# Hybrid decoder block on one core: the mean square of x taken from the transposed x

## What is computed

```
def rmsnorm(x, w):
    return x * rsqrt(mean(x * x, axis=-1) + EPS) * w      # x: 256 tokens x 1024

h = rmsnorm(x, norm_mix)
proj = h @ w_in          # split: q, six kv heads, gates, retention q ("qr"), k, v, ...
```

## Time and profile before

| | |
|---|---|
| time, median of 3 (lowest, highest) | 472.08 us (471.12, 472.64) |
| span of the profiled execution | 469.9 us |
| TensorE busy | 438.6 us, 93% |
| VectorE busy | 193.7 us, 41% |
| ScalarE busy | 76.9 us, 16% |
| GpSimd busy | 23.4 us, 5% |
| moved by DMA | 150.79 MB, mean 321 GB/s |

### The profile page before, as it was taken

How to read it: one execution, slowest core, us unless ns; L and a number is a source line. 1 busy time by engine, 2 the same in 40 slices (tenths; PEclk the granted TensorE clock), 3 DMA queues, 4 the chain that set the end, 5 groups by cost and what they waited for, 6 DMA issues and landing times.

```text
span 469.9 us, 5881 instructions
## 1 busy us (share of the span) xinstructions
PE 438.6 (93%) x2326; PEld 241.9 (51%) x2326; DVE 193.7 (41%) x430; ACT 76.9 (16%) x209; POOL 23.4 (5%) x44
## 2 busy tenths in 40 slices
PE   8999999999999999999999998999999767958983
PEld 7799885555455555454444775353543421413331
DVE  1683047836975758778831243110201100200113
ACT  1000131423062111110012341010110100101113
POOL 2020000310000010100002110000000000000000
PEclk9999999999999999999999999999999995996998
DMA  8999557508407107969499899999999999999993
GB/s 286 425 423 366 198 173 310 227 0 339 199 0 280 78 1 280 412 270 424 179 389 423 340 369 375 420 430 434 415 436 427 416 431 421 435 430 425 423 413 117
DMA packets 25388, 150.79 MB, mean 321 GB/s; under 512 B 5484, under 2 KB 7949, under 8 KB 18446
## 3 DMA queue, kind: packets, MB, share of 16 engines
q1 hardware_dynamic: 19152, 145.02, 75.0%
q10 hardware_dynamic: 6206, 5.36, 3.5%
HBM read 147.75 MB, written 2.62 MB: 320 GB/s over the span
## 4 chain that ended last, share of the span: by engine, by line
PE 82%; DMA 14%; DVE 1%; ACT 1%; issue 1%; ACTq 0%; SPq 0%; DVEq 0%; POOL 0%
PE bank L741 34%; PE bank L716 33%; DMA spare<-in_moe_gate_up 7%; DMA ring<-in_moe_gate_up 5%; PE bank L1164 5%; PE bank L1146 4%; PE bank L747 2%; PE bank L796 2%; DMA ring<-in_dense 2%; ACT nsa L1597 1%; PE bank L1303 1%; ACT cst L1597 0%; DVE hT_and_y L2213 0%; DVE nsa L2144 0%; PE bank L1215 0%
## 5 line engine op out<-in xcount | busy, mean ns | idle before, releaser
L741 PE MATMUL bank<-ring,x 128*128 128x512 f32 x128 | 57.4, 594 | 0.0
L2153 DVE SCALAR_TENSOR_TENSOR wr<-cst,bank 128x256 f32<-128x256 f32 x8 | 3.4, 421 | 98.2 <-ACT cst L1604 98.2
L741 PE MATMUL bank<-ring,hT_and_y 128*128 128x512 f32 x96 | 43.5, 597 | 0.0
L716 PE MATMUL bank<-ring,nsa 128*32 128x512 f32 x304 | 38.1, 641 | 4.7 <-DMA ring<-in_moe_gate_up 4.3
L716 PE MATMUL bank<-hT_and_y,ring 128*128 128x256 f32 x192 | 42.3, 380 | 0.0
L1164 PE MATMUL bank<-selection,Tb 128*128 128x128 f32 x256 | 33.7, 284 | 5.9 <-ACT cst L1597 5.8
L716 PEld LDWEIGHTS bank<-hT_and_y,ring 128*128 128x128 f32 x192 | 36.2, 190 | 5.7 <-DVE hT_and_y L1690 0.6
L1164 PEld LDWEIGHTS bank<-selection,Tb 128*128 128x128 f32 x256 | 30.4, 194 | 15.8 <-issue 15.7
L741 PEld LDWEIGHTS bank<-ring,x 128*128 128x128 f32 x128 | 23.8, 190 | 27.1 <-issue 27.0
L2144 DVE COPY nsa<-bank 128x512 f32<-128x512 f32 (+1 forms) x20 | 12.5, 625 | 56.0 <-PE bank L1164 30.5
L741 PEld LDWEIGHTS bank<-ring,hT_and_y 128*128 128x128 f32 x96 | 17.6, 190 | 20.3 <-issue 20.3
(11 more groups left out here) (258 smaller groups left out, 625.6 us busy)
## 6 DMA issues: line engine op xcount, KB each, us to landing
ring<-in_moe_gate_up SPq DMA_DIRECT2D x18, 2048.0 KB, 18.3
ring<-in_dense SPq DMA_DIRECT2D x17, 2048.0 KB, 9.1
spare<-in_moe_gate_up SPq DMA_DIRECT2D x4, 2048.0 KB, 20.2
hT_and_y<-in_moe_gate_up SPq DMA_DIRECT2D x4, 2048.0 KB, 23.2
vr_and_gr<-in_moe_gate_up SPq DMA_DIRECT2D x3, 2048.0 KB, 24.8
nsa<-in_moe_down SPq DMA_DIRECT2D x11, 512.0 KB, 15.1
windows<-in_moe_down SPq DMA_DIRECT2D x7, 512.0 KB, 14.4
qkT<-in_moe_down SPq DMA_DIRECT2D x7, 512.0 KB, 14.8
```

What stands on the lines that cost most here:

```text
L716: return nc.tensor.matmul(o, l, r, start=s, stop=e)
L741: ins = nc.tensor.matmul(o, l[:, k, :], r[:, k, :], start=first and k == 0, stop=last and k == n - 1, skip_group_check=True)
```

## The change

The load of x at the start is left out; only the later one is left. The mean square comes from xT instead:

- ScalarE squares each part of xT as it lands, with scale 1/32 before squaring (so the 1024 squares add up to a mean), into `xT_squared`, 8 chunks of 256 columns in the region that holds v later. The first three stand before the small loads of ACT's queue, the last two after them.
- VectorE adds the eight chunks to one in four instructions: chunks 2-3 onto 0-1, 6-7 onto 4-5, 4-5 onto 0-1, 1 onto 0. The first stands between its weighting of parts 3 and 4, the other three after that of part 4.
- TensorE sums over the partitions by token: two matmuls with the summed squares as weights and one column of ones (job `ms`, put in bank 0 outside the turn). They stand before k=5. `R` stands before k=7, as before.
- VectorE adds EPS while it takes `ms` from PSUM; GpSimd's `rstd(0)` waits for that and now stands before its copy of the bias table's rows.
- `xw` is written to a region of its own, so xT stays as it is; `diag` moves to the other half of its region.

```diff
@@ -93,7 +93,7 @@
-JOBS = (["qr0", "R", "qr1", "btab"]
+JOBS = (["qr0", ("ms", 0), "R", "qr1", "btab"]
         + ["kvcT", "ksT", "vs", "kwT", "vwg", "qT0", "qT1"]
@@ -133,8 +133,13 @@
 LAST_N = [0] * NBANK
-for _i, _job in enumerate(JOBS):
-    _b = (_i + BANK0) % NBANK
+_i = 0
+for _job in JOBS:
+    if isinstance(_job, tuple):
+        _job, _b = _job
+    else:
+        _b = (_i + BANK0) % NBANK
+        _i += 1
     if _job is None:
@@ -291,9 +296,11 @@
         squared = pair_a[:, 2048:4096].rearrange("p (t d) -> p t d", t=TT)
-        xw = Tb[:, :].rearrange("p (k t) -> p k t", k=KT)
+        xT = Tb[:, :].rearrange("p (k t) -> p k t", k=KT)
+        xw = pair_a[:, 2048:4096].rearrange("p (k t) -> p k t", k=KT)
+        xT_squared = pair_b[:, 0:2048].rearrange("p (k t) -> p k t", k=KT)
         x_squared = cst[:, C_ROT + D:C_ROT + D + 512]
-        diag = vr[:, 0, 0:TT * P]
+        diag = gr[:, 0, 0:TT * P]
         h_sums = x[:, :, :].rearrange("p t (s k n) -> p (t s) k n", s=2, k=4)
@@ -302,6 +309,7 @@
         s_first = [sem(f"first_block_part{i}") for i in range(len(FIRST))]
+        s_xsq, s_xadd = sem("xT_part_squared"), sem("xT_squares_added")
         s_xw, s_diag, s_ones, s_h = sem("x_weighted"), sem("rstd_diagonal"), sem("ones_ready"), sem("h_ready")
@@ -467,9 +475,6 @@
             for i, ks in enumerate(FIRST):
-                if i == len(FIRST) - 1:
-                    for t in range(TT):
-                        sp.dma_start(x[:, t, :], a["x"][0, t * P:(t + 1) * P, :]).then_inc(s_x[t], 16)
                 w = slice(KT + ks[0] * S if i else 0, KT + (ks[-1] + 1) * S)
@@ -627,9 +632,7 @@
-            def rstd(n, col):
-                pool.wait_ge(s_rs, n)
+            def rstd(col):
                 pool.tensor_tensor(st[:, col + 32:col + 34], st[:, col:col + 2],
@@ -638,9 +641,10 @@
             pool.memset(Pc[:, :, :, :], NEG).then_inc(s_ms, 1)
+            pool.wait_ge(*is_emptied("ms"))
+            rstd(0)
             pool.wait_ge(s_tab, 32)
             pool.tensor_copy(relb_rep, relb.unsqueeze(2).broadcast_to((BUCKETS + 1, HEADS, P // HEADS))).then_inc(s_rep, 1)
-            rstd(1, 0)
             pool.wait_ge(*is_emptied("kvcT"))
...
@@ -797,18 +802,27 @@
                         done(f"qr{i}", ins)
+            def token_squares():
+                o = begin("ms")
+                pe.wait_ge(s_xadd, 4)
+                for t in range(TT):
+                    ins = mm(o[:, t:t + 1], xT_squared[:, 0, t * P:(t + 1) * P], ones[:, 0:1], True, True)
+                done("ms", ins)
+            def spread_rstd():
+                o = begin("R")
+                for t in range(TT):
+                    pe.wait_ge(s_diag, t + 1)
+                    ins = mm(o[:, t * P:(t + 1) * P], ones[:, :], diag[:, t * P:(t + 1) * P], True, True)
+                done("R", ins)
             for i, ks in enumerate(FIRST):
...
                 for k in ks:
-                    if k < KT - 1:
-                        raw_queries(k)
-            o = begin("R")
-            pe.wait_ge(s_ones, 1)
-            for t in range(TT):
-                pe.wait_ge(s_diag, t + 1)
-                ins = mm(o[:, t * P:(t + 1) * P], ones[:, :], diag[:, t * P:(t + 1) * P], True, True)
-            done("R", ins)
-            raw_queries(KT - 1)
+                    if k == 5:
+                        token_squares()
+                    if k == KT - 1:
+                        spread_rstd()
+                    raw_queries(k)
@@ -1377,11 +1391,20 @@
+            def xT_squares(i):
+                ks = slice(FIRST[i][0], FIRST[i][-1] + 1)
+                act.wait_ge(s_xT[i], 16)
+                nc.scalar.activation(xT_squared[:, ks, :], xT[:, ks, :], ACT.Square, scale=D ** -0.5).then_inc(s_xsq, 1)
+            for i in range(3):
+                xT_squares(i)
             act.wait_ge(s_first[2], 16)
...
             act.dma_start(relb[0:BUCKETS, :], a["rel_bias"]).then_inc(s_tab, 16)
+            for i in range(3, len(FIRST)):
+                xT_squares(i)
             o = take("btab")
@@ -1670,16 +1693,23 @@
                 for k in FIRST[i]:
-                    tsc(xw[:, k, :], xw[:, k, :], norm_cols[:, k:k + 1], None, ALU.mult, ALU.bypass).then_inc(s_xw, 1)
-            for i in range(len(FIRST) - 1):
+                    tsc(xw[:, k, :], xT[:, k, :], norm_cols[:, k:k + 1], None, ALU.mult, ALU.bypass).then_inc(s_xw, 1)
+            def add_squares(k, n, m):
+                V.tensor_tensor(xT_squared[:, k:k + n, :], xT_squared[:, k:k + n, :], xT_squared[:, m:m + n, :], ALU.add).then_inc(s_xadd, 1)
+            for i in range(4):
                 weighted_x(i)
-            for t in range(TT):
-                dve.wait_ge(s_x[t], 16)
-                ins = V.tensor_tensor_reduce(gr[:, t, :], x[:, t, :], x[:, t, :], 1.0, 0.0, ALU.mult, ALU.add,
-                                             st[:, 200 + t:201 + t])
-            link(ins)
-            tsc(st[:, 0:2], st[:, 200:202], 1.0 / D, EPS, ALU.mult, ALU.add).then_inc(s_rs, 1)
-            weighted_x(len(FIRST) - 1)
+            dve.wait_ge(s_xsq, 3)
+            add_squares(0, 2, 2)
+            weighted_x(4)
+            dve.wait_ge(s_xsq, len(FIRST))
+            add_squares(4, 2, 6)
+            dve.wait_ge(s_xadd, 2)
+            add_squares(0, 2, 4)
+            dve.wait_ge(s_xadd, 3)
+            add_squares(0, 1, 1)
+            o = take("ms")
+            freed("ms", tsc(st[:, 0:2], o[:, 0:2], EPS, None, ALU.add, ALU.bypass))
             dve.wait_ge(s_rstd, 1)
@@ -2043,7 +2073,7 @@
                 take(piece)
-                dve.wait_ge(s_x[t], 32)
+                dve.wait_ge(s_x[t], 16)
                 xx = x[:, t, c0:c1]
```

More of the change, by code:

```diff
@@ L675, in _ @@
             for i in range(4):
-                rstd(2 + i, 8 + 4 * i)
+                pool.wait_ge(s_rs, i + 1)
+                rstd(8 + 4 * i)
             def weighted(piece):
@@ L682, in router_rstd @@
             def router_rstd(t):
-                pool.wait_ge(s_rs, 6 + t)
+                pool.wait_ge(s_rs, 5 + t)
                 pool.tensor_tensor(st[:, 36 + t:37 + t], st[:, 4 + t:5 + t], st[:, 250:251], ALU.pow).then_inc(s_rstd, 1)
@@ L693, in _ @@
             for t in range(TT):
-                pool.wait_ge(s_rs, 8 + t)
+                pool.wait_ge(s_rs, 7 + t)
                 pool.tensor_tensor(st[:, 38 + t:39 + t], st[:, 6 + t:7 + t], st[:, 250:251], ALU.pow).then_inc(s_rstd, 1)
```

## The result

The changed kernel takes 473.00 us at the median (471.97 to 475.27), the kernel before 472.59 in the runs beside it; the ratio is 1.0022, with a 95% interval of 1.0012 to 1.0032. The medians lie 0.4 us apart, the means of the runs (473.3 and 472.4) 0.9. The ratio makes it 1.04 us more (0.6 to 1.5), which lies within the 0.3% that the prediction called no change, and on the side it gave. The execution profiled took 473.11 us, with a span of 471.3; the one of before had a span of 469.9.

The account below looks back on a forecast made before the run. TensorE's chain (82% of the span) was taken as the bound. Standstill, `ms` and the removed gap put k=6 at 17.29 instead of 16.29 us, +1.00; span 469.9 + 1.0 = 470.9, plus 2.2 outside it: 473.1 us, range 471.2 to 474.7.

Parts of the forecast that it names:

- TensorE's chain, read in the first 22 us: All edits lie before 22 us on TensorE's chain; the shift there, +1.00 us, passes whole to the end.
- Where the last xT part lands: Behind part four on SP's queue: lands at 10.30 + 2.11 = 12.41 us, bounds 12.2 and 12.8.
- Square and adds: After the last xT part: ScalarE's square 0.60 us, then VectorE's three adds 0.72 + 0.72 + 0.42, to 14.97 us.
- The standstill: TensorE, before `ms` and k=5, waits 0.82 us for the adds, from 14.20 to 15.02 us.
- The removed half: Early x loads, square sums and scaling go: VectorE's 0.36 us gap before k=6 goes; sooner landings costed at nothing.
- From `ms` to R: Scaling, GpSimd's power and diagonals, 1.87 us before, hide under k=5 and 6: diagonals at 17.4, wanted at 19.0.
- GpSimd's order: Power before the copy of the bias table: 16.4 us without an engine's delay, bias product due at 21.2; covered.
- Rival B: Bias table late: 13 small rows an engine behind 16 KB rows, 20.6 us against 21.2 due; up to 474.5; chance 0.04.
- Rival A: Squares later still, TensorE waits longer before k=5: last xT part after 12.83 us; middle 474.3; chance 0.20.
- Rival C: No standstill before k=5, squares in time (landing by 11.6 us, or shorter adds): +0.18 us, 472.1; chance 0.12.
- Rival E: TensorE's clock falls to 1.2 GHz after the standstill; k=5 and 6 need 3.4 us more: 476.5; chance 0.04.
- Rival D: DMA as a whole sets the end, so 1 MB less saves 2.5 us: 469.6; chance 0.05.

Follow-up runs that it names:

- e3: The kernel before with 23 products of ones (46 records) added before k=5; ratio to the kernel before 1.0102 (1.0079 to 1.0125).
- e5: The kernel before without the early loads of x and the sums of squares, mean squares set to 1; ratio to the kernel before 1.0111 (1.0079 to 1.0144).
- e8: The changed kernel with GpSimd's copy of the bias table put before the power again; ratio to the kernel before 1.0065 (1.0040 to 1.0090).
- e10: As e5, with the three small loads on SP's queue, behind the identity and ahead of kv0; ratio to the kernel before 0.9997 (0.9984 to 1.0010).
- e2: The changed kernel with `ms` before k=4 in place of k=5; ratio to the kernel before 1.0067 (1.0041 to 1.0093).
- e4: The changed kernel with x's two early loads kept, behind the last part of xT on SP's queue; ratio to the kernel before 1.0010 (0.9990 to 1.0031).
- e1: The changed kernel with `ms` before k=6 in place of k=5; ratio to the kernel before 1.0009 (0.9994 to 1.0025).
- e6: The changed kernel with R before k=6 in place of k=7; ratio to the kernel before 1.0014 (0.9993 to 1.0035).
- e7: As e5, with the three small loads issued ahead of the fifth weight part on ACT's queue; ratio to the kernel before 1.0058 (1.0039 to 1.0077).

## Why the prediction was right, point by point

- **The number.** Forecast 473.1, measured 473.0: that close is luck. The kernel before had a median of 472.08 in the three runs that the forecast started from and of 472.59 in the 22 beside the changed kernel; and of the 1.04 us of the ratio (forecast 1.00) the front accounts for 0.54. Right are the side, the place and the size within a factor of two. By its own words the prediction would be wrong if TensorE had no wait before k=5, and two of five profiles have none.
- **TensorE's chain, read in the first 22 us.** Right: all of the change that can be placed lies there, and e3 shows that a shift there reaches the end. The profiles of e5 and e8 don't match their ratios as well (3.2 us at the front against 3.7 to 6.8, and 4.8 against 1.9 to 4.3), as each is one execution of six.
- **Where the last xT part lands.** Forecast 12.41, measured 11.99 (12.07, 12.12 and 12.03 in the three that wait), and this is most of what was off in the end of the adds, 14.97 against 14.54. The parts came 1.92 us apart (10.07 to 11.99), which is the 1.9 us that the shares gave; the text had the right arithmetic and then took 2.11 from the row of another pair. Part four was also 0.23 sooner than before.
- **Square and adds.** Right: 0.63 for 0.60, three adds in 1.88 for 1.86.
- **`ms`.** From its first weight load at 14.59 to k=5 at 15.09 are 0.50 us, forecast 0.54. k=6 came at 15.09 + 1.73 = 16.82, 0.53 after the 16.29 of the earlier trace rows. That is the 0.54 us of the first projection. The forecast 15.56 for k=5 is 0.47 more, of which the landing is 0.42. In this one profile TensorE itself was there no sooner, so an even earlier landing would have won nothing.
- **The standstill.** Forecast 0.82, measured none in two profiles and 0.20 to 0.54 in three, with k=5 at nearly the same place: what counts is when the adds are through or TensorE is there, whichever is later, and not how long TensorE stood. The start's pace, which the earlier trace rows doesn't show, decides how much of it is seen. Adding a measured standstill to the length of TensorE's work would mislead here.
- **The removed half.** VectorE's hold on k=6 is gone (0.36 us in the first profile of the kernel before, 0.24 in the second), as forecast. What that is worth depends on the start: R at 17.36 (e10) or, but for its pause, 18.0 (e5), against 18.09 before. R at 18.63 in the changed kernel then puts the added half at 1.27 us in an execution that starts like e10's and at 0.6 in one like e5's. The hold on k=2 until 9.01, which the prediction kept, isn't part of it: the second profile of the kernel before has none.
- **From `ms` to R.** Right that it hides: 15.5 to 16.7 (forecast 17.4), under k=5 and 6. From R to the first projection are 3.18 us before, after and in e10, so nothing changed there. The prediction's 0.2 us by which hT is late against the bias product is less than 0.1: the earlier trace rows has hT through at 21.22, and TensorE's chain goes on at 21.27.
- **GpSimd's order.** Wrong in its price. It was costed at nothing, and the copy of the table was looked at only for the bias product's sake. In fact the change itself pushes the copy from 15.95 to 19.67, and without the new order the power would be behind it (e8: 3.1 us over the kernel before in place of about 1). The new order isn't free of effect: it saves some 2 us.
- **Rival B** had the mechanism right: 13 small rows beside 16 KB rows, forecast 20.6, measured 19.6. It misses the bias product (20.89) by under a microsecond, as forecast. What it didn't ask is who else stands behind that landing.
- **Rival A** didn't happen (the part would have had to land 0.84 later than it did). **Rival C**, no standstill, did happen in two profiles, but not by its way: the squares weren't sooner than 11.6 us, TensorE was late. **Rival E** is real in the executions profiled with 2.24 and 2.58 us of standstill (e8, e2), absent with 3.03 (e5), and absent at 0.5. **Rival D**: the 2.5 us for the missing 1 MB are not won at the end (e10: at most 0.8).

**What stays open.** The ratio is 1.04 us up (0.6 to 1.5), the front 0.54, so the rest may be as little as 0.1. In the profiles the expert stage, where DMA is busy without a break, lies further back than the front explains. TensorE waits there for `vr_and_gr` (start, us, what, idle before); first the kernel before, its second profile, then the changed kernel:

```profile
...
367.74 1.92 PE L716 MATMUL bank<-vr_and_gr,nsa 128*32 128x512 f32 x16 [2.02 <-DMA vr_and_gr<-in_moe_gate_up]
...
```

```profile
...
368.34 1.92 PE L716 MATMUL bank<-vr_and_gr,nsa 128*32 128x512 f32 x16 [2.71 <-DMA vr_and_gr<-in_moe_gate_up]
...
```

```profile
...
369.06 3.35 PE L721 MATMUL bank<-vr_and_gr,nsa 128*32 128x512 f32 x16 [2.79 <-DMA vr_and_gr<-in_moe_gate_up]
...
```

The changed kernel is 1.32 us later, 0.78 of it beyond its front. But the second profile of the kernel before is 0.60 us later than the first, though its front is 0.09 earlier: two equal kernels differ by 0.7 here. Over all profiles, what this wait is late beyond the shift of the last dense products is 0, 0.70, -0.09 and -0.63 us with x's early load (before twice, e3, e4), and 0.78, 0.41, 0.64, 0.59, 1.62, 1.09, 0.54, 0.62 and 0.23 without it (the changed kernel twice, e1, e2, e5, e6, e7, e8, e10): a mean of 0.0 over four against 0.72 over nine. That speaks for theory 2, that the sooner and smaller DMA traffic costs some tenths of a microsecond where the expert stage begins, but with that spread and one variant only that keeps the load beside the change, it isn't shown. The ratios of e4 (1.0010) and the changed kernel (1.0022, 1.0017) don't separate it either. No mechanism for it was found.

## What to carry to other kernels

When a transfer is taken out ahead of a large one, the large one moves up beside all small transfers of the other queue; look up who waits for those, and who stands behind that wait on the same engine. A wait put into a busy engine's order is priced by the moment at which it is met, against where the work stood before, not by the length of the idle time it shows. And a pause can cost more than its length: those of 2.24 and 2.58 us here were followed by products at half pace, though one of 3.03 us wasn't. Where an engine's start differs from execution to execution, as TensorE's does here, comparing one profile of each kernel can be off by half a microsecond (0.65 us between e5 and e10); compare two that start alike, or several.

## What the runs showed of the hardware

- Two queues share the DMA engines by count of rows, not by bytes: 2 KB rows beside 4 KB rows got 0.26 MB through in 1.92 us at 420 GB/s, a third; 13 rows of at most 1.5 KB beside 16 KB rows needed some 7 us (the copy at 19.67 in place of 15.95, 16.43 with x's load kept and 12.99 with the loads ahead of kv0). *The Trainium skill, "DMA: Bandwidth & Descriptors", "Queues, rings and completion order", has the turns go by packets of several descriptors, typically 9 to 17; the trace of the changed kernel doesn't agree with packets that large: the 128 rows of `vecT`, 8 an engine if they are spread evenly over 16, moved from 12.5 to 17.0 us, which is about one row of 16 KB (0.61 us in the trace) for each small one.*
- TensorE's pace doubles at a moment of its own after the start, from before 5 to about 7 us, and an execution that has it late gets through 5 records of the first query products where another gets through 8.
- After standstills of 2.58 us (e2) and 2.24 us (e8) the granted clock fell to about 0.5, for some 3 and some 7 us; after 3.03 us (e5) and after 0.54 us (e4) it stayed at 1.00. The length of the pause alone doesn't tell.
- GpSimd's power takes 0.70 us for 2 columns and 41.15 us for 256.
